# A two-model decoder kernel: VectorE's top-k laid in four parts between groups of four expert dots, and the next head's query matmuls laid between the value sets of an earlier sum

## Chip, cores and metric

One Trainium2 chip, one core of it. The metric is the time of one execution on the device in microseconds (us), lower is better. A change of this kernel under about 0.3% cannot be told from none.

## What is computed

A first model of two layers (attention, a pooling mixer and a PEER feed-forward) is followed by a second one of four layers (three kinds of attention and a squared-ReLU MLP). There are 256 tokens of width 1024, all in fp32. The change touches PEER alone, the product-key expert layer of the two first layers:

```python
def one_block(xblk):                                   # 128 tokens, two blocks
    q = (xblk @ w_query).reshape(B, 128, 8, 2, 256)    # 8 heads
    s = jnp.einsum('bthpd,hpnd->bthpn', q, sub_keys)   # 128 keys for each half
    vals, idx = lax.top_k(s, 16)
    cand = vals[..., 0, :, None] + vals[..., 1, None, :]      # 16 x 16
    cand_idx = idx[..., 0, :, None] * 128 + idx[..., 1, None, :]
    top_s, pos = lax.top_k(cand.reshape(B, 128, 8, 256), 16)
    eidx = jnp.take_along_axis(cand_idx.reshape(B, 128, 8, 256), pos, axis=-1)
    g = jax.nn.softmax(top_s, axis=-1)
    h = jnp.einsum('btd,bthkd->bthk', xblk, expert_u[eidx])
    act = jax.nn.gelu(h, approximate=False) * g
    return jnp.einsum('bthk,bthkd->btd', act, expert_v[eidx])
```

Each token, head and rank takes one row of `expert_u` and one of `expert_v`, 4 KB each.

## The kernel before, in words

The kernel is written engine by engine, with semaphores between them and all orders set by hand. Every engine takes its instructions in the order in which they are written.

PEER works in chunks. A chunk is one head h and one block t of 128 tokens, so a layer has 16 chunks; below, chunk c is 2h + t. The two chunks of a head use one half j of the buffers each, in a loop whose body holds two heads.

**GpSimd (POOL)** issues the gathers. `u_rows` (L1805) brings four U rows for each of the 128 tokens as four indirect DMAs of 512 KB; `v_rows` (L1818) does that for a V set of four ranks. The order is U group 0 of chunk c, V set 0 of chunk c-1, U group 1, V set 1 and so on: 32 gathers in a chunk. Only eight U buffers exist, so a U group waits until the dots of two groups earlier are done (`h_ready`). A V set waits until TensorE has used the same set of the chunk before (`v_free`).

**VectorE (DVE)** runs `dots`: 16 dots (L1575), each when its rows have landed; then it waits for ScalarE's exponential (`gate_ready`) and its gelu (`gelu_ready`), multiplies them (L1582), spreads the weights over the partitions (L1584, `rw_ready`) and copies the next index table (L1566). Then comes `topk` for the chunk two further on: for t = 0 a copy of the scores out of PSUM (L1520), two top-16 searches over 128 keys, the 16 x 16 sums and a top-16 search over them, and the arithmetic of the expert number (L1542 to L1552), which releases GpSimd's U rows of that chunk (`idx_ready`). At the end `stationaries` (L1597) builds the weight columns for TensorE out of `weights_by_pair`.

**TensorE (PE)** runs, for head h, `weights_by_pair` (L771) and `expert_sum` (L784, four sets of 16 matmul passes, each set when its V rows have landed) for t = 0, then `weights_by_pair` for t = 1, then `query` of head h+2, then `expert_sum` for t = 1. `query` transposes the sub-keys (L736), multiplies tokens by the head's query weights in four groups of 16 passes (L744), waits for ScalarE's copy of the result and makes the key scores (L751, `ps_done`).

**ScalarE (ACT)** runs `query_copies` (L1036 the transposed keys, L1038 the query after `q_done`) and `expert_weights` (L1044 the exponential, L1047 the gelu). `query_copies(h+1)` stands ahead of both `expert_weights` of head h, in one queue.

**SyncE (SP)** loads the query weights (2048 KB) and sub-keys (256 KB) of a head once those of two heads earlier are used.

Of the kernel before, what the change touches and what calls it, by code (L numbers as in the profile page):

```python
# [26 lines left out]
ALU = mybir.AluOpType  # L27
# [3 lines left out]
P = 128  # L31
D = 1024
S = 256
NT = S // P
KC = D // P
# [10 lines left out]
PH = 8  # L46
# [147 lines left out]
def program(nc, T, out):  # L194
    with ExitStack() as ctx:
# [354 lines left out]
        def _(pe):  # L550
# [110 lines left out]
            with pe.Fori(0, DEPTH) as l:  # L661
# [65 lines left out]
                def query(h, j, first):  # L727
# [12 lines left out]
                    for b in (2, 3, 0, 1):  # L740
                        if b == 0:
                            wait_loop(pe, sk_used, h + 1)
                        for k in range(KC):
                            mm = pe.matmul(psT[:, b // 2, (b % 2) * S:(b % 2 + 1) * S], ring[:, j, k, b * P:(b + 1) * P],  # L744
                                           xT[:, k, :], start=(k == 0), stop=(k == KC - 1))
                    mm.then_inc(q_done, 1)
# [7 lines left out]
                    mm.then_inc(ps_done, 1)  # L754

# [17 lines left out]
                def expert_sum(h, j, t, ahead=True):  # L773
# [4 lines left out]
                    for s in range(NSET):  # L778
# [8 lines left out]
                        mm.then_inc(v_free, 1)  # L787

                query(0, 0, True)
# [12 lines left out]
                query(1, 1, False)  # L802
                with pe.Fori(0, PH // 2 - 1) as hp:
                    for j in range(2):
                        weights_by_pair(2 * hp + j, j, 0)
                        expert_sum(2 * hp + j, j, 0)
                        weights_by_pair(2 * hp + j, j, 1)
                        query(2 * hp + 2 + j, j, False)
                        expert_sum(2 * hp + j, j, 1)
# [127 lines left out]
        def _(act):  # L937
# [61 lines left out]
            with act.Fori(0, DEPTH) as l:  # L999
# [49 lines left out]
                query_copies(0)  # L1049
                with act.Fori(0, PH // 2 - 1) as hp:  # L1050
                    query_copies(2 * hp + 1)
                    for t in range(NT):
                        expert_weights(2 * hp, 0, t)
                    query_copies(2 * hp + 2)
                    for t in range(NT):
                        expert_weights(2 * hp + 1, 1, t)
                query_copies(PH - 1)
# [127 lines left out]
        def _(dve):  # L1185
# [244 lines left out]
            with dve.Fori(0, DEPTH) as l:  # L1430
# [84 lines left out]
                def topk(h, j, t):  # L1515
                    cb = NT * j + t
                    restart_chain()
                    if t == 0:
                        wait_loop(dve, ps_done, h + 1)
                        link(dve.tensor_copy(topb[:, :, 0, :], psS[:, 1, :].rearrange("p (a n) -> p a n", n=NKEY)))  # L1520
                        dve.sem_inc(ps_used, 1)
                    for q in range(2):
                        top16(topb[:, 2 * t + q, 0, :], topb[:, 2 * t + q, 1, :], NKEY, vals[:, q, :], idxu[:, q, :])
                    link(dve.tensor_copy(idxf[:, :, :], idxu[:, :, :]))
# [11 lines left out]
                    link(dve.tensor_tensor(m(0), down(vals[:, 0, :]), along(vals[:, 1, :]), ALU.add))  # L1536
                    if not (isinstance(h, int) and h < 2):

                        wait_loop(dve, v_free, h * 8 + (4 * t - 8), alone=True)
                    top16(sc2[:, 0, :], sc2[:, 1, :], 256, tops[:, cb, :], posu[:, 0, :])  # L1540
                    link(dve.tensor_scalar(nmx[:, cb, :], tops[:, cb, 0:1], -1.0, None, ALU.mult))
# [26 lines left out]
                def dots(h, j, t, ahead=True):  # L1568
# [3 lines left out]
                    for k in range(TOPK):  # L1572
# [3 lines left out]
                                                 ALU.mult, ALU.add, hdot[:, cb, k:k + 1]).then_inc(h_ready, 1)  # L1576

# [8 lines left out]
                    if ahead:  # L1586
                        take_indices(c + 1, cb + 1)

# [21 lines left out]
                with dve.Fori(0, PH // 2 - 1) as hp:  # L1610
                    for j in range(2):
                        for t in range(NT):
                            dots(2 * hp + j, j, t)
                            topk(2 * hp + j + 1, 1 - j, t)
                            stationaries(2 * hp + j, j, t)
                for t in range(NT):
                    dots(PH - 2, 0, t)
                    topk(PH - 1, 1, t)
                    stationaries(PH - 2, 0, t)
                for t in range(NT):  # L1620
                    dots(PH - 1, 1, t, ahead=(t == 0))
# [237 lines left out]
```

## Time and profile before

| | |
|---|---|
| time, median of 3 runs | 3718.97 us (3710.23 to 3719.86) |
| the profiled execution: time, span | 3713.7 us, 3711.8 us |
| busy: PE, DVE, ACT, POOL | 2547.4, 2080.9, 827.9, 1119.8 us |
| DMA over the span | 884.64 MB, 238 GB/s |
| indirect gathers: instructions, bytes of their queue | 1024, 536.94 MB |
| first and last U gather, layer one | 343.74 us, 1068.05 us |
| first U gather, layer two | 1455.99 us |

The busy times are sums over stages that have nothing in common. Only the two PEER stages, some 750 us each, hold the work that is moved here; GpSimd has no instruction of weight outside them. So they are read by themselves, in windows and in the timelines of single engines. A row of a timeline gives the start, the duration, the engine, the line, the operation, its tiles and, in brackets, how long the engine stood idle before it and what ended that.

### The profile page before, as it was taken

To read this page: it belongs to the slowest core of one execution; us is meant where nothing else is said; L and a number is where in the kernel's file an instruction comes from. 1 tells how busy PE (TensorE), PEld (TensorE's weight loads), DVE (VectorE), ACT (ScalarE), POOL (GpSimd) and SP (SyncE) were. 2 spreads that over 40 slices of the span, in tenths; PEclk is the share of its full clock that TensorE was granted. 3 is DMA by queue.
4 is the path that set the end of the run, shared out by engine and by line. 5 is a ranking of instruction groups with operands and counts; after the bars stand their busy time and mean duration, and the time that the engine had idled before them with its cause. 6 is when DMAs were issued, how large, how long until landed. Compare 5 with 4: busy or idle time off the path is not lost.

```text
span 3711.8 us, 34410 instructions
## 1 busy us (share of the span) xinstructions
PE 2547.4 (69%) x12111; PEld 1746.3 (47%) x12111; DVE 2080.9 (56%) x4572; ACT 827.9 (22%) x1271; POOL 1119.8 (30%) x1028
## 2 busy tenths in 40 slices
PE   5986444444345986444444337799889979989898
PEld 2454222222002444222222005589778967977697
DVE  4544666667634545666666634655445554555554
ACT  0110100000000110100000004344434433444343
POOL 0001777677760001777777750000000000000000
PEclk9998776677556998776677568699969976998699
DMA  7723999999987713999999985145414531544153
GB/s 287 281 72 113 371 386 373 384 374 379 367 330 254 281 71 118 374 382 372 384 379 372 383 314 189 38 162 195 148 38 159 191 115 46 181 172 146 46 181 125
DMA packets 306600, 884.64 MB, mean 238 GB/s; under 512 B 21192, under 2 KB 31520, under 8 KB 306336
## 3 DMA queue, kind: packets, MB, share of 16 engines
q0 software_dynamic: 147456, 536.94, 37.9%
q1 hardware_dynamic: 159008, 346.05, 26.0%
q8 instruction: 66, 1.08, 0.1%
q14 instruction: 70, 0.57, 0.0%
HBM read 881.86 MB, written 1.05 MB: 238 GB/s over the span
## 4 chain that ended last, share of the span: by engine, by line
PE 48%; POOL 19%; DVE 13%; issue 13%; DMA 4%; ACT 2%; SPq 1%; DVEq 0%; POOLq 0%; ACTq 0%
POOL proj L1805 9%; PE lin L576 8%; PE lin L829 6%; PE lin L830 6%; PE lin L831 6%; POOL ring L1818 5%; POOL vbuf L1818 4%; PE psS L613 3%; DMA proj<-in_expert_u,eidx 2%; DVE proj L1575 2%; PE lin L642 2%; PE psT L556 2%; PE psT L829 2%; PE psT L830 2%; PE psT L831 2%
## 5 line engine op out<-in xcount | busy, mean ns | idle before, releaser
L1575 DVE CUSTOM_DVE_ANT_0 proj<-proj,tokb 128x1024 f32<-128x1024 f32 x512 | 611.1, 1224 | 410.9 <-DMA proj<-in_expert_u,eidx 384.7
L1805 POOL DMA_INDIRECT proj<-in_expert_u,eidx x512 | 545.1, 1065 | 927.3 <-DVEq L1553 704.9
L1282 DVE TENSOR_TENSOR weights_split<-ring,weights_split 128x1024 fp32r<-128x1024 f32 (+1 forms) x376 | 451.8, 1208 | 515.4 <-ACT weights_split L1093 514.9
L784 PE MATMUL lin<-ring,rowb 128*32 128x512 f32 x896 | 225.9, 1032 | 523.7 <-DMA ring<-in_expert_v,pT 302.8
L1093 ACT ACTIVATE weights_split<-ring 128x1024 fp32r<-128x1024 f32 (+1 forms) x376 | 391.7, 1046 | 570.3 <-PE lin L831 357.5
L784 PE MATMUL lin<-vbuf,rowb 128*32 128x512 f32 x1024 | 186.1, 871 | 260.4 <-DMA vbuf<-in_expert_v,pT 153.4
L784 PEld LDWEIGHTS lin<-ring,rowb 128*32 128x32 f32 x896 | 37.1, 157 | 669.2 <-DMA ring<-in_expert_v,pT 312.6
L576 PE MATMUL lin<-ring,xT 128*128 128x512 f32 x768 | 342.4, 607 | 5.6 <-DVE xT L1234 3.4
L1818 POOL DMA_INDIRECT vbuf<-in_expert_v,pT x256 | 293.1, 1145 | 78.1 <-issue 77.8
L1818 POOL DMA_INDIRECT ring<-in_expert_v,pT x224 | 249.3, 1113 | 68.3 <-issue 67.7
L576 PEld LDWEIGHTS lin<-ring,xT 128*128 128x128 f32 x768 | 148.8, 195 | 192.4 <-issue 184.7
L1047 ACT ACTIVATE gel<-hdot 128x16 f32<-128x16 f32 x32 | 6.9, 216 | 1013.1 <-DVE hdot L1575 1013.1
L744 PE MATMUL psT<-xT,ring 128*128 128x256 f32 x1024 | 228.9, 385 | 0.0
L829 PE MATMUL lin<-weights_split,act_split 128*128 128x512 f32 x512 | 202.6, 396 | 14.2 <-DVE act_split L1757 14.2
L744 PEld LDWEIGHTS psT<-xT,ring 128*128 128x128 f32 x1024 | 197.8, 195 | 27.1
L784 PEld LDWEIGHTS lin<-vbuf,rowb 128*32 128x32 f32 x1024 | 34.7, 139 | 370.4 <-DMA vbuf<-in_expert_v,pT 284.8
L830 PE MATMUL lin<-weights_split,act_split 128*128 128x512 f32 x512 | 201.9, 394 | 0.0
L831 PE MATMUL lin<-weights_split,act_split 128*128 128x512 f32 x512 | 201.9, 394 | 0.0
L829 PE MATMUL lin<-weights_split,xT_high 128*128 128x512 f32 (+1 forms) x480 | 190.4, 397 | 13.0 <-DVE xT_low L1299 7.4
L830 PE MATMUL lin<-weights_split,xT_low 128*128 128x512 f32 (+1 forms) x480 | 188.5, 393 | 0.0
L831 PE MATMUL lin<-weights_split,xT_high 128*128 128x512 f32 (+1 forms) x480 | 187.7, 391 | 0.0
L829 PE MATMUL psT<-xT_high,weights_split 128*128 128x256 f32 x512 | 148.8, 291 | 0.0
(236 smaller groups left out, 4590.8 us busy)
## 6 DMA issues: line engine op xcount, KB each, us to landing
ring<-in_mlp_w_up SPq DMA_DIRECT2D x32, 2048.0 KB, 8.1
ring<-in_mlp_w_down SPq DMA_DIRECT2D x32, 2048.0 KB, 7.6
ring<-in_ada_w SPq DMA_DIRECT2D x24, 2048.0 KB, 13.1
ring<-in_w_in SPq DMA_DIRECT2D x16, 2048.0 KB, 12.0
ring<-in_w_query SPq DMA_DIRECT2D x16, 2048.0 KB, 13.1
ring<-in_diff_w_in SPq DMA_DIRECT2D x12, 2048.0 KB, 8.0
ring<-in_moba_w_in SPq DMA_DIRECT2D x6, 2048.0 KB, 8.2
ring<-in_w_attn_o SPq DMA_DIRECT2D x4, 2048.0 KB, 11.7
```

Source lines behind the costliest of these rows:

```text
L576: mm = pe.matmul(lin[:, pair + t, 0:cols], lhs[:, k, t * P:(t + 1) * P], rhs[:, k, :], start=(k == 0), stop=(k == kc - 1))
L613: mm = pe.matmul(psS[:, g % 2, t * S:t * S + n], qkT[lo:hi, qb, t * P:(t + 1) * P], qkT[lo:hi, kb, 0:n], start=True, stop=True)
L744: mm = pe.matmul(psT[:, b // 2, (b % 2) * S:(b % 2 + 1) * S], ring[:, j, k, b * P:(b + 1) * P], xT[:, k, :], start=(k == 0), stop=(k == KC ...
L784: mm = pe.matmul(lin[32 * b:32 * b + 32, 2 * half + t, :], wst[:, cb % 2, 4 * b + s, :], vrow(SETROWS * s + b)[:, half * 512:(half + 1) * ...
L829: pe.matmul(out_ap, lhs[0], rhs[0], start=first, stop=False, skip_group_check=True)
L830: pe.matmul(out_ap, lhs[1], rhs[0], start=False, stop=False, skip_group_check=True)
L831: return pe.matmul(out_ap, lhs[0], rhs[1], start=False, stop=last, skip_group_check=True)
L1093: act.activation(part(p, 0, kind, w), raw_piece(slot, p, kind, w), ACT.Copy).then_inc(hi_ready, 1)
L1282: dve.tensor_tensor(part(p, 1, kind, w), raw_piece(slot, p, kind, w), part(p, 0, kind, w).bitcast(F32), ALU.subtract).then_inc(lo_ready, 1)
L1575: dve.tensor_tensor_reduce(ubuf[:, n % GB, :], ubuf[:, n % GB, :], tokb[:, t, :], 1.0, 0.0, ALU.mult, ALU.add, hdot[:, cb, k:k + 1]).then_ ...
L1805: pool.indirect_dma_start(out=ubuf[:, (16 * cb + k) % GB, :], out_offset=None, in_=table["u"], in_offset=bass.IndirectOffsetOnAxis(ap=eidx ...
L1818: pool.indirect_dma_start(out=vrow(SETROWS * s + b), out_offset=None, in_=table["v"], in_offset=bass.IndirectOffsetOnAxis(ap=eidxT[:, cb % ...
```

## The change

`topk` becomes `topk_part`, in four parts. Part 0 is the copy of the scores (t = 0 only) and the first search over 128 keys, part 1 the second search, part 2 the 16 x 16 sums with their search, part 3 the arithmetic of the expert number. `dots` calls part 0 after the 4th dot, part 1 after the 8th, part 2 after the 12th, and part 3 after the weights are spread. `query` becomes `query_keys`, `query_rows` in four parts and `key_scores`. The loop on TensorE calls `query_keys(h+2)` ahead of `expert_sum` of t = 0, one part of `query_rows` after each V set of that sum, and `key_scores` behind it: that is one chunk earlier than before. On ScalarE `query_copies(h+2)` moves between the two `expert_weights` of head h. GpSimd's and SyncE's orders stay as they are. The numbers of instructions and bytes stay too.

```diff
-                def query(h, j, first):
+                def query_keys(h, j):
...
-                    for b in (2, 3, 0, 1):
-                        if b == 0:
-                            wait_loop(pe, sk_used, h + 1)
-                        for k in range(KC):
-                            mm = pe.matmul(psT[:, b // 2, (b % 2) * S:(b % 2 + 1) * S], ring[:, j, k, b * P:(b + 1) * P],
-                                           xT[:, k, :], start=(k == 0), stop=(k == KC - 1))
-                    mm.then_inc(q_done, 1)
+
+                def query_rows(h, j, part):
+
+                    b = (2, 3, 0, 1)[part]
+                    if part == 2:
+                        wait_loop(pe, sk_used, h + 1)
+                    for k in range(KC):
+                        mm = pe.matmul(psT[:, b // 2, (b % 2) * S:(b % 2 + 1) * S], ring[:, j, k, b * P:(b + 1) * P],
+                                       xT[:, k, :], start=(k == 0), stop=(k == KC - 1))
+                    if part == 3:
+                        mm.then_inc(q_done, 1)
+
+                def key_scores(h):
+
                     wait_loop(pe, q_used, h + 1)
...
-                def expert_sum(h, j, t, ahead=True):
+                def expert_sum(h, j, t, ahead=True, asked=False):
...
                         mm.then_inc(v_free, 1)
+                        if asked:
+                            query_rows(h + 2, j, s)
...
                         weights_by_pair(2 * hp + j, j, 0)
-                        expert_sum(2 * hp + j, j, 0)
+                        query_keys(2 * hp + 2 + j, j)
+                        expert_sum(2 * hp + j, j, 0, asked=True)
+                        key_scores(2 * hp + 2 + j)
                         weights_by_pair(2 * hp + j, j, 1)
-                        query(2 * hp + 2 + j, j, False)
                         expert_sum(2 * hp + j, j, 1)
...
                 query_copies(0)
+                query_copies(1)
                 with act.Fori(0, PH // 2 - 1) as hp:
-                    query_copies(2 * hp + 1)
-                    for t in range(NT):
-                        expert_weights(2 * hp, 0, t)
-                    query_copies(2 * hp + 2)
-                    for t in range(NT):
-                        expert_weights(2 * hp + 1, 1, t)
-                query_copies(PH - 1)
+                    for j in range(2):
+                        expert_weights(2 * hp + j, j, 0)
+                        query_copies(2 * hp + 2 + j)
+                        expert_weights(2 * hp + j, j, 1)
...
                                                  ALU.mult, ALU.add, hdot[:, cb, k:k + 1]).then_inc(h_ready, 1)
+                        if ranked and k % 4 == 3 and k < 12:
+                            topk_part(h + 1, 1 - j, t, k // 4)
...
                     if ahead:
                         take_indices(c + 1, cb + 1)
+                    if ranked:
+                        topk_part(h + 1, 1 - j, t, 3)
...
                             dots(2 * hp + j, j, t)
-                            topk(2 * hp + j + 1, 1 - j, t)
                             stationaries(2 * hp + j, j, t)
```

How it moves instructions, in the order of each queue (an fp32 matmul is one row there and two passes in the profile, so x8 here is x16 there):

**ScalarE**, in the loop, from the gelu of block t = 0 to that of t = 1 and the query copies; `gel` is the gelu, `eg` the exponential, `sm<-psT` the copy of the query. Before:

```order
L1047 ACTIVATE gel<-hdot 128x16
L410 REGISTER_ALU
L1044 ACT_TABLE_LOAD
L1044 ACTIVATE eg,ers<-tops,nmx 128x16
L410 ISA
L1047 ACT_TABLE_LOAD
L1047 ACTIVATE gel<-hdot 128x16
L410 REGISTER_ALU
L1036 ACTIVATE pT<-psT 128x512
L1038 ACTIVATE sm<-psT 128x1024
```

The change:

```order
L1064 ACTIVATE gel<-hdot 128x16
L410 REGISTER_ALU x2
L1053 ACTIVATE pT<-psT 128x512
L1055 ACTIVATE sm<-psT 128x1024
L410 REGISTER_ALU
L1061 ACT_TABLE_LOAD
L1061 ACTIVATE eg,ers<-tops,nmx 128x16
L410 ISA
L1064 ACT_TABLE_LOAD
L1064 ACTIVATE gel<-hdot 128x16
```

The two copies, which followed the gelu of t = 1, now precede the exponential and the gelu of t = 1.

**TensorE**, in the loop, at the end of the sum of t = 0; `psT<-xT,ring` is the query, `lin<-...,rowb` a V set, `psS<-pT,sm` the key scores. Before:

```order
L771 MATMUL psS<-const,pT 128x16
L410 ISA
L736 MATMUL psT<-const,ring 128x128 x4
L410 REGISTER_ALU
L744 MATMUL psT<-xT,ring 128x256 x16
L410 REGISTER_ALU
L744 MATMUL psT<-xT,ring 128x256 x16
L751 MATMUL psS<-pT,sm 128x128 x8
L410 REGISTER_ALU
L784 MATMUL lin<-vbuf,rowb 32x512 x16
```

The change:

```order
L798 MATMUL lin<-ring,rowb 32x512 x8
L410 REGISTER_ALU
L747 MATMUL psT<-xT,ring 128x256 x8
L798 MATMUL lin<-ring,rowb 32x512 x3
L798 MATMUL lin<-pr,rowb 32x512
L798 MATMUL lin<-ring,rowb 32x512 x3
L798 MATMUL lin<-pr,rowb 32x512
L747 MATMUL psT<-xT,ring 128x256 x8
L758 MATMUL psS<-pT,sm 128x128 x8
L785 MATMUL psS<-const,pT 128x16
```

The last quarter of the query now follows the last V set of t = 0, and the weights of t = 1 (L785) follow the key scores.

**VectorE**, in the loop, from the 4th dot of t = 0 to the 5th; before, the 5th dot followed the 4th at once:

```order
L1598 ISA hdot 128x1
L1215 ISA
L410 REGISTER_ALU
L1539 COPY rope_t<-psS 128x4x128
L1524 MAX vals<-rope_t 128x8
L1525 MAX_INDEX idxu<-vals,rope_t 128x8
L1526 MATCH_REPLACE rope_t<-vals,rope_t 128x128
L1527 MAX vals<-rope_t 128x8
L1528 MAX_INDEX idxu<-vals,rope_t 128x8
L1598 ISA proj,hdot<-proj,tokb 128x1024
```

The copy of the scores has moved from behind the 16 dots to behind four of them.

## Rows read from the trace of the kernel before

**Rows 1.** Page, costliest groups: the dots and the U gathers.
```profile
L1575 DVE CUSTOM_DVE_ANT_0 proj<-proj,tokb 128x1024 f32<-128x1024 f32 x512 | 611.1, 1224 | 410.9 <-DMA proj<-in_expert_u,eidx 384.7
L1805 POOL DMA_INDIRECT proj<-in_expert_u,eidx x512 | 545.1, 1065 | 927.3 <-DVEq L1553 704.9
```
**Rows 2.** Busy time by windows (count), granted clock, DMA share, GB/s: two loops, one unranked chunk.
```profile
426.14:985.96 559.82, 260.50 (x1320) 123.31 (x1320) 374.44 (x931) 47.67 (x72) 423.76 (x384) 0.67 0.99 377
1042.79:1074.81 32.02, 10.92 (x48) 1.78 (x48) 18.29 (x31) 0.00 (x0) 24.70 (x25) 0.50 1.02 410
1554.60:2110.00 555.40, 256.24 (x1290) 118.78 (x1288) 373.45 (x929) 50.04 (x75) 422.17 (x384) 0.67 0.99 378
```
**Rows 3.** Line view of L1805, its wait for the dots, and of L1818, its landing times.
```profile
  DVE hdot L1575: 70.6, 12
...
DMA to landing us min/median/max: 5.2/6.5/12.9
```
**Rows 4.** Timeline of GpSimd, 547 to 662 us.
```profile
547.03 1.14 POOL L1805 DMA_INDIRECT proj<-in_expert_u,eidx  x1 [5.93 <-DVE hdot L1575]
...
578.41 0.97 POOL L1818 DMA_INDIRECT vbuf<-in_expert_v,pT  x1 [0.30 <-issue]
...
589.17 1.99 POOL L1818 DMA_INDIRECT vbuf<-in_expert_v,pT  x1 [0.30 <-issue]
...
615.74 0.99 POOL L1818 DMA_INDIRECT pr<-in_expert_v,pT  x1 [0.30 <-issue]
...
660.65 0.94 POOL L1818 DMA_INDIRECT pr<-in_expert_v,pT  x1 [0.31 <-issue]
```
**Rows 5.** Timeline of TensorE, 622 to 644 us: last set of t = 0, query, key scores.
```profile
622.81 1.07 PE L784 MATMUL lin<-ring,rowb 128*32 128x512 f32 x3 [9.29 <-DMA pr<-in_expert_v,pT]
...
626.95 13.98 PE L744 MATMUL psT<-xT,ring 128*128 128x256 f32 x64
642.04 2.05 PE L751 MATMUL psS<-pT,sm 128*128 128x128 f32 x16 [1.11 <-ACT sm L1038]
```
**Rows 6.** Timeline of ScalarE, 617 to 645 us.
```profile
617.23 0.22 ACT L1047 ACTIVATE gel<-hdot 128x16 f32<-128x16 f32 x1 [41.63 <-DVE hdot L1575]
...
640.97 1.02 ACT L1038 ACTIVATE sm<-psT 128x1024 f32<-128x1024 f32 x1 [13.22 <-PE psT L744]
642.01 1.28 ACT L1044 ACT_TABLE_LOAD   x1
643.30 0.31 ACT L1044 ACTIVATE eg<-tops,nmx 128x16 f32<-128x16 f32 x1
...
643.72 1.28 ACT L1047 ACT_TABLE_LOAD   x1
```
**Rows 7.** Timeline of VectorE, 572 to 588 us: weights, top-k from copy to end, dots.
```profile
572.72 0.23 DVE L1582 SCALAR_TENSOR_TENSOR actw<-eg,ers,gel 128x16 f32<-128x16 f32 x1 [0.30 <-ACT gel L1047]
...
573.28 0.69 DVE L1520 COPY rope_t<-psS 128x512 f32<-128x512 f32 x1
...
581.54 0.32 DVE L1542 TENSOR_SCALAR posu<-posu 128x16 uint32<-128x16 uint32 x1
...
586.24 0.68 DVE L1597 TENSOR_TENSOR rowb<-const,psS 128x512 f32<-128x512 f32 x1
586.84 1.22 DVE L1575 CUSTOM_DVE_ANT_0 proj<-proj,tokb 128x1024 f32<-128x1024 f32 x1
```
**Rows 8.** Timelines at the start of layer one's PEER: GpSimd.
```profile
363.81 1.68 POOL L1805 DMA_INDIRECT proj<-in_expert_u,eidx  x1 [10.21 <-DVE hdot L1575]
...
371.09 0.94 POOL L1805 DMA_INDIRECT proj<-in_expert_u,eidx  x1 [0.30 <-issue]
...
404.11 1.68 POOL L1805 DMA_INDIRECT proj<-in_expert_u,eidx  x1 [6.18 <-DVE hdot L1575]
```
**Rows 9.** Timeline of TensorE there: the key scores of head 1.
```profile
376.82 2.05 PE L751 MATMUL psS<-pT,sm 128*128 128x128 f32 x16 [1.11 <-ACT sm L1038]
```
**Rows 10.** Timeline of TensorE, 655 to 676 us: the last set of t = 1.
```profile
671.62 1.08 PE L784 MATMUL lin<-ring,rowb 128*32 128x512 f32 x3 [7.00 <-DMA pr<-in_expert_v,pT]
```

More of the change, by code:

```diff
@@ L754, in query @@
                     mm.then_inc(ps_done, 1)
+                def query(h, j):
+                    query_keys(h, j)
+                    for part in range(4):
+                        query_rows(h, j, part)
+                    key_scores(h)
                 def indices_by_pair(c, cb):
@@ L787, in expert_sum @@
                         mm.then_inc(v_free, 1)
-                query(0, 0, True)
+                        if asked:
+                            query_rows(h + 2, j, s)
+                query(0, 0)
                 for t in range(NT):
@@ L801, in _ @@
                 indices_by_pair(1, 1)
-                query(1, 1, False)
+                query(1, 1)
                 with pe.Fori(0, PH // 2 - 1) as hp:
@@ L1515, in topk, with topk_part @@
                 def topk(h, j, t):
+                    for part in range(4):
+                        topk_part(h, j, t, part)
+                def topk_part(h, j, t, part):
                     cb = NT * j + t
                     restart_chain()
-                    if t == 0:
+                    if t == 0 and part == 0:
                         wait_loop(dve, ps_done, h + 1)
@@ L1521, in topk @@
                         dve.sem_inc(ps_used, 1)
-                    for q in range(2):
+                    if part < 2:
+                        q = part
                         top16(topb[:, 2 * t + q, 0, :], topb[:, 2 * t + q, 1, :], NKEY, vals[:, q, :], idxu[:, q, :])
-                    link(dve.tensor_copy(idxf[:, :, :], idxu[:, :, :]))
+                        return
                     grid = [P, TOPK, TOPK]
@@ L1534, in m @@
                         return sc2[:, q, :].rearrange("p (a b) -> p a b", a=TOPK)
[L1536 to L1541, printed above, removed]
+                    if part == 2:
+                        link(dve.tensor_copy(idxf[:, :, :], idxu[:, :, :]))
+                        link(dve.tensor_tensor(m(0), down(vals[:, 0, :]), along(vals[:, 1, :]), ALU.add))
+                        if not (isinstance(h, int) and h < 2):
+                            wait_loop(dve, v_free, h * 8 + (4 * t - 8), alone=True)
+                        top16(sc2[:, 0, :], sc2[:, 1, :], 256, tops[:, cb, :], posu[:, 0, :])
+                        link(dve.tensor_scalar(nmx[:, cb, :], tops[:, cb, 0:1], -1.0, None, ALU.mult))
+                        return
                     link(dve.tensor_scalar(posu[:, 1, :], posu[:, 0, :], 4, None, ALU.logical_shift_right))
@@ L1566, in take_indices, with dots @@
                     dve.tensor_copy(eidxT[:, cb % 4, :], idx_at(cb)).then_inc(it_used, 1)
-                def dots(h, j, t, ahead=True):
+                def dots(h, j, t, ahead=True, ranked=True):
                     cb = NT * j + t
@@ L1617, in _ @@
                     dots(PH - 2, 0, t)
-                    topk(PH - 1, 1, t)
                     stationaries(PH - 2, 0, t)
                 for t in range(NT):
-                    dots(PH - 1, 1, t, ahead=(t == 0))
+                    dots(PH - 1, 1, t, ahead=(t == 0), ranked=False)
                     stationaries(PH - 1, 1, t)
```

## The prediction, made before the changed kernel ran

> **What bounds the kernel now.** I read the line groups of the page first, then windows over the two PEER loops, then the timelines of the single engines in one head. The page's busy shares mislead: they mix stages. The windows [rows 2] cut out chunks 2 to 13 of layer one, six heads, and as many gathers of layer two: 384 gathers each, in 559.82 and 555.40 us. The DMA share there is 0.99 at 377 GB/s, TensorE is busy for under half, VectorE for 67%. Two resources are near their end. One is DMA: in the chunk without top-k it moves 410 GB/s [rows 2], 1.28 us for a gather's 524 KB. A head brings 64 gathers, 2.10 MB of query weights and 0.26 MB of sub-keys, 35.9 MB, which at 410 GB/s take 87.6 us. The other is GpSimd, which issues the gathers one by one: 0.94 us and 0.30 us of "issue" [rows 4], 1.24 us each, 79.4 us a head. A head takes more than either:
>
> - layer one: 559.82 / 6 = 93.3 us. GpSimd's busy time is 423.76 - 384 x 0.94 = 62.8 us over plain issues, 10.5 a head. What is left after 384 x 0.30 is 20.9 us, 3.5 a head, in which it waits for dots.
> - layer two: 92.6 = 79.4 + 10.2 + 3.0, in the same way.
>
> So a head is 93.0 us: **79.4 of issues, 10.3 of stretched issues, 3.3 of waits**. GpSimd's queue is the path; all 12 of its waits for dots come to 70.6 us [rows 3].
>
> The stretches stand beside dots alone: the issue at 578.41 takes 0.97 us in the middle of the top-k, that at 589.17 takes 1.99 us after the dots have begun again at 586.84 [rows 4, 7]. They are worst when the top-k, 13 us in one piece (573.28 to 586.24) [rows 7], has let rows pile up and eight dots run on end. The waits come from that piece as well: 5.93 us at 547.03 [rows 4]. In the unranked chunk 25 issues hold only 24.70 - 25 x 0.94 = 1.2 us of stretch [rows 2], since there each dot follows its landing.
>
> **What the change does to it, part by part.**
>
> *Top-k in four parts.* No instruction is added but three restarts of the step counter a chunk, which hide in VectorE's idle third. Parts of 1.8 to 4.7 us after four dots of 4.6 us fit into the 10 us from one U group to the next, so in steady flow the dots keep to the landings. The waits for dots (3.3 us a head) go. The stretches fall, between two ends: not at all (10.3), and to the unranked chunk's rate, 1.2 / 25 x 64 = 3.1 us. I take 7.5. It is nearer the upper end because, as the next point shows, each head still has three groups of four dots run on end, and part 3 with the stationaries leaves one late group.
>
> The Trainium skill, SBUF — State Buffer, "Who interferes with whom", says that a VectorE instruction with two SBUF inputs contends with a GpSimd instruction that reads SBUF, and that the loser blocks for the whole instruction. The 1.99 us beside a 1.22 us dot agree with it [rows 4, 1]. Taken by itself it speaks against this change, since there are as many dots as before. That is the rival "stretches stay" below, and the unranked chunk is the row against it.
>
> *Query between the V sets, and ScalarE's queue.* Here I see the price. The exponential and the gelu of block t = 1 now stand behind the copy of the query of head h+2, which waits for the last quarter of the query, which stands behind the last V set of t = 0. That set's gathers are issued after the last U group of t = 1. So VectorE finishes the 16 dots of t = 1 and stands at `gate_ready`. Counted from the end of the last V issue (615.74 + 0.99 = 616.7 [rows 4]):
>
> 1. the set begins at 622.81 [rows 5]: 6.1 us. Bounds: 5.2 us from issue to landing at the least [rows 3], so 4.2, and 671.62 - 661.6 = 10.0 [rows 10, 4];
> 2. set: 3.6 us (622.81 to about 626.4); quarter of the query: 13.98 / 4 = 3.5 us at 2.4 GHz [rows 5]. A set of 3.6 us goes with a granted clock of 0.50, 1.2 GHz, in the unranked chunk [rows 2], so the quarter begins at that level: I add 0.5. Sum 7.6; bounds 5.3 (both at 2.4 GHz) and 10.6 (both at 1.2 GHz);
> 3. ScalarE: from 640.93, the query's end, to the end of a gelu behind it: copy 1.02, table load 1.28, exponential with its accumulator 0.4, table load 1.28 (from 643.72), gelu 0.22 [rows 6]: 4.3 us. Before, the gelu was at 617.23, right after the last dot;
> 4. VectorE: weights 0.56 (572.72 to 573.28), part 3 4.7 (581.54 to 586.24), stationaries 0.6, four dots 4.6 [rows 7]: 10.5 us. Then 0.2 us to GpSimd.
>
> Together 28.7 us. GpSimd meanwhile has two U groups and two V sets to issue, 16 x 1.24 + 0.3 = 20.1 us, with some stretch 20.8; its third U group of the next chunk needs those four dots. **It waits 7.9 us, once a head**, for heads 0 to 5, whose sums carry a query: six times a layer. Bounds: 4.2 + 5.3 + 15.0 - 20.8 = 3.7 us, and 10.0 + 10.6 + 15.0 - 20.8 = 14.8 us. I take 7.9, the values of one head's own rows.
>
> The same rows weigh a rule. In them the exponential starts at 643.30, directly behind its load of 1.28 us [rows 6]. The Trainium skill, ScalarE: Activation LUTs, "What ACT_TABLE_LOAD costs", adds a drain of 1380 ns to each. By it the two loads of step 3 would cost 2.8 us more a head, 33 us in all; the row shows no drain, and my sum has none.
>
> After the wait VectorE works off its arrears: copy of the scores and part 0, part 1 and part 2 with four dots each. GpSimd's next third of a head is 20 us long, so I find no second wait. The key scores are ready about 17 us after the reference point, before part 0 asks. `weights_by_pair` of t = 1 falls into part 3. SyncE's query load starts some 10 us earlier than before and is wanted 90 us later: nothing.
>
> Head: 79.4 + 7.5 + 7.9 = 94.8 us, against 93.0: **+1.8 x 12 = +21.6 us**.
>
> *The start of a layer.* Part 0 for head 1 now follows the first four dots, while TensorE ends the key scores of head 1 only at 376.82 + 2.05 = 378.9 [rows 9]. The four dots are done at 363.5, as GpSimd's release at 363.81 shows [rows 8]. VectorE waits 15 us; copy, part 0 and four dots end at 386.3. GpSimd's fourth U group, at 371.1 before, comes at 386.4. From there: group 0 of chunk 1 after part 1 and four dots (392.8), V set 0, group 1 (402.8), V set 1, to 412.9 for group 2, which stood at 404.11 and there still had a wait of 6.18 us in it [rows 8]. +8.8 us a layer, **+17.6 us**.
>
> *The end of a layer.* Some one and a half ranked chunks with no wait, before and after: 3 us less stretch a layer, **-6 us**.
>
> Sum: 21.6 + 17.6 - 6 = +33 us. The profiled execution took 3713.7 us (span 3711.8), 5 us under the median of the runs and inside their spread. That gives **3747 us**, +0.9%. A change under about 0.3% (11 us) a measurement of this kernel cannot tell from none.
>
> **Rivals.**
>
> - *Faster: the flow smooths out.* If TensorE, busier and more even, keeps 2.4 GHz, the set and quarter take 5.3 us; if also the last set begins nearer its minimum, the wait is about 5.0, and with stretches at 5.0 a head is 89.4, still over DMA's 87.6. Then 12 x -3.6 + 17.6 - 6 = -32: 3682 us. It decides once wait and stretch together are under 11.7 us a head. For it: the unranked chunk, and 13 us in one piece gone. Against: ScalarE's order.
> - *No change.* TensorE at 2.4 GHz alone: wait 5.6, head 92.5, 12 x -0.5 + 11.6 = +6: 3719 us.
> - *Stretches stay* at 10.3: head 97.6, +67: 3780 us. For it: no dot is gone, and arrears make bursts.
> - *TensorE stays at 1.2 GHz* through the query quarter: 3.0 us more wait, head 97.8, +69: 3783 us; with the last set as late as in rows 10, 3.9 more each, 3830 us. Against: the granted clock is up in every query of the timeline.
> - *The drain of the page* on top: 3780 us, though the trace has none.
>
> **How the numbers follow.** Forecast (3747, by itself 3725 to 3770) 0.31; smooth flow 0.26; no change 0.17; stretches stay 0.15; low clock 0.08; drain 0.03. Faster 0.26, within 0.3% 0.17, slower 0.57. For 8 in 10 the range reaches down towards the smooth case and up over the two cases at 3780: 3688 to 3800 us.
>
> **What would show it.** In the profile after: GpSimd waits for dots about six times a layer, some 8 us each, always ahead of the third U group of an even chunk; VectorE waits some 10 us for ScalarE's gate or gelu after the last dot of odd chunks; on ScalarE the exponential directly follows the query copy; mean issue 1.05 us where it is 1.10; U group 3 of chunk 0 some 15 us late in each layer. Wrong if the gelu of odd chunks comes within 2 us of the last dot, if GpSimd has no such waits, or if its issues are stretched as before.

## The result, and the profile after

| | before | after |
|---|---|---|
| time, median | 3717.95 us | 3787.95 us (4 runs, 3781.62 to 3792.93) |
| ratio, 95% interval | 1 | 1.0193 [1.0175, 1.0212] |
| profiled execution: time, span | 3713.7, 3711.8 us | 3792.9, 3791.0 us |

Slower, as forecast, but by 70 us where 33 were worked out (3747 us); the range up to 3800 us holds it. The page after, costliest groups, beside [rows 1]:

```profile
L1830 POOL DMA_INDIRECT proj<-in_expert_u,eidx x512 | 533.6, 1042 | 1035.1 <-DVEq L1576 700.5
L1598 DVE CUSTOM_DVE_ANT_0 proj<-proj,tokb 128x1024 f32<-128x1024 f32 x512 | 611.4, 1224 | 243.0 <-DMA proj<-in_expert_u,eidx 212.0
```

The U issues got shorter (1042 ns for 1065) and their idle time grew by 108 us. The window over chunks 2 to 13 of layer one, columns as in [rows 2]:

```profile
439.00:1025.64 586.64, 268.43 (x1272) 116.72 (x1270) 369.33 (x929) 50.27 (x75) 409.06 (x385) 0.70 0.95 359
```

By this window a head takes 97.8 us where it took 93.3; the DMA share is down from 0.99 to 0.95, and the granted clock is up from 0.67 to 0.70. The view of waits lists for whom GpSimd waits (total us, times, longest):

```profile
POOL proj L1830 <- DVE hdot L1598: 184.5, 18, 17.7
POOL proj L1830 <- issue: 150.1, 492, 0.3
```

Its waits for dots grew from 70.6 us [rows 3] to 184.5. I cut GpSimd's timeline into the start of a layer (first gather to U group 2 of chunk 1), six heads (to U group 2 of chunk 13) and the rest. Stretch is what the issues take over 0.94 us; wait is what a head takes beyond its stretch and 64 x 1.24 us:

| us, layer one / two | before | after | forecast of the difference |
|---|---|---|---|
| start | 60.4 / 59.4 | 74.3 / 74.2 | +8.8 |
| a head | 93.05 / 93.0 | 98.0 / 97.8 | +1.8 |
| of it stretch | 10.2 / 10.6 | 8.2 / 7.9 | -2.8 |
| of it wait | 3.5 / 3.0 | 10.4 / 10.5 | +4.6 |
| rest | 131.1 / 129.2 | 124.9 / 129.9 | -3 |

Heads bring +58.5 us (forecast 21.6), starts +28.7 (17.6), rests -5.5 (-6). Together 81.7, of which the span shows 79.2.

The hold that was forecast, VectorE standing still for ScalarE's exponential and gelu, is there as described. VectorE, GpSimd, TensorE and ScalarE around the end of chunk 5, each from its own timeline:

```profile
636.76 1.23 DVE L1598 CUSTOM_DVE_ANT_0 proj<-proj,tokb 128x1024 f32<-128x1024 f32 x1
...
650.47 0.16 DVE L1605 RECIPROCAL ers<-ers 128x1 f32<-128x1 f32 x1 [12.48 <-ACT eg L1061]
651.88 0.23 DVE L1607 SCALAR_TENSOR_TENSOR actw<-eg,ers,gel 128x16 f32<-128x16 f32 x1 [1.25 <-ACT gel L1064]
...
657.42 1.22 DVE L1598 CUSTOM_DVE_ANT_0 proj<-proj,tokb 128x1024 f32<-128x1024 f32 x1
```

```profile
635.38 0.93 POOL L1843 DMA_INDIRECT pr<-in_expert_v,pT  x1 [0.31 <-issue]
...
662.89 0.93 POOL L1830 DMA_INDIRECT proj<-in_expert_u,eidx  x1 [6.71 <-DVE hdot L1598]
```

```profile
641.89 0.63 PE L798 MATMUL lin<-ring,rowb 128*32 128x512 f32 x3 [1.75 <-DMA pr<-in_expert_v,pT]
...
643.75 3.72 PE L747 MATMUL psT<-xT,ring 128*128 128x256 f32 x16
648.58 2.05 PE L758 MATMUL psS<-pT,sm 128*128 128x128 f32 x16 [1.11 <-ACT sm L1055]
```

```profile
647.50 1.02 ACT L1055 ACTIVATE sm<-psT 128x1024 f32<-128x1024 f32 x1 [45.60 <-PE psT L747]
648.54 1.28 ACT L1061 ACT_TABLE_LOAD   x1
649.84 0.31 ACT L1061 ACTIVATE eg<-tops,nmx 128x16 f32<-128x16 f32 x1
...
651.55 0.22 ACT L1064 ACTIVATE gel<-hdot 128x16 f32<-128x16 f32 x1
```

But GpSimd's wait is not the same in each head. In layer one it is 6.68 and 6.71 us at chunks 2 and 6, 8.13 at 10 and 12, and twice as much at chunks 4 and 8: 16.30 and 16.34 us. Two of them, at chunks 4 and 10:

```profile
568.35 0.94 POOL L1830 DMA_INDIRECT proj<-in_expert_u,eidx  x1 [16.30 <-DVE hdot L1598]
...
860.95 0.94 POOL L1830 DMA_INDIRECT proj<-in_expert_u,eidx  x1 [8.13 <-DVE hdot L1598]
```

From the end of the last V issue to the end of the gelu 15.5 to 17.2 us pass in each of the twelve heads. From there to the gather it is 19.3 to 19.5 us at chunks 4 and 8 of both layers, and 10.8 to 11.4 us at the other eight. Chunk 4, VectorE's timeline:

```profile
554.11 0.68 DVE L1624 TENSOR_TENSOR rowb<-const,psS 128x512 f32<-128x512 f32 x1
560.14 1.22 DVE L1598 CUSTOM_DVE_ANT_0 proj<-proj,tokb 128x1024 f32<-128x1024 f32 x1 [5.35 <-issue]
...
565.10 0.08 DVE L1598 DVE_READ_ACCUMULATOR2_ANT hdot<- 128x1 f32 x1 [2.58 <-issue]
```

"issue" means that VectorE waited for nothing that the profile shows. At chunk 6 the dots follow the stationaries at once (657.42 above); here 5.35 and 2.58 us pass without an instruction. Chunks 4 and 8 open the second and the third pass of VectorE's loop over pairs of heads. The kernel before had the first gap at the same place, but not the second: its dots run on end.

```profile
541.55 1.23 DVE L1575 CUSTOM_DVE_ANT_0 proj<-proj,tokb 128x1024 f32<-128x1024 f32 x1 [5.33 <-issue]
```

The first four dots end at 546.2 and release the wait of 5.93 us at 547.03 that [rows 4] show, which I had put down to the top-k.

### The profile page after: what moved, and what is told of

The parts are those of the page before. It is cut to its first block, busy times and chain, and to the rows that moved or that the text cites. A ratio compares the mean times of both kernels' runs of the same rounds, so it can differ in the third digit from the quotient of the medians.

```text
span 3791.0 us, 34574 instructions
## 1 busy us (share of the span) xinstructions
PE 2584.4 (68%) x12111; PEld 1752.9 (46%) x12111; DVE 2071.3 (55%) x4572; ACT 828.6 (22%) x1271; POOL 1089.5 (29%) x1028
## 4 chain that ended last, share of the span: by engine, by line
PE 49%; POOL 20%; issue 14%; DVE 11%; DMA 3%; ACT 2%; SPq 0%; POOLq 0%; DVEq 0%; ACTq 0%
POOL proj L1830 9%; PE lin L576 8%; POOL ring L1843 6%; PE lin L846 6%; PE lin L847 6%; PE lin L848 6%; POOL vbuf L1843 4%; PE psT L747 3%; PE psS L613 3%; DMA pr<-in_expert_v,pT 2%; PE lin L642 2%; PE psT L556 2%; PE psT L846 2%; PE psT L847 2%; PE psT L848 2%
## 5 line engine op out<-in xcount | busy, mean ns | idle before, releaser
L1830 POOL DMA_INDIRECT proj<-in_expert_u,eidx x512 | 533.6, 1042 | 1035.1 <-DVEq L1576 700.5
L798 PE MATMUL lin<-ring,rowb 128*32 128x512 f32 x896 | 216.5, 994 | 446.2 <-DMA ring<-in_expert_v,pT 258.8
L798 PE MATMUL lin<-vbuf,rowb 128*32 128x512 f32 x1024 | 214.6, 988 | 320.8 <-DMA vbuf<-in_expert_v,pT 264.7
L576 PE MATMUL lin<-ring,xT 128*128 128x512 f32 x768 | 338.5, 601 | 5.8 <-DVE xT L1249 3.4
L798 PEld LDWEIGHTS lin<-ring,rowb 128*32 128x32 f32 x896 | 36.0, 150 | 569.1 <-DMA ring<-in_expert_v,pT 267.3
L1843 POOL DMA_INDIRECT vbuf<-in_expert_v,pT x256 | 262.6, 1026 | 78.1 <-issue 77.8
L1843 POOL DMA_INDIRECT ring<-in_expert_v,pT x224 | 261.8, 1169 | 68.3 <-issue 68.3
L747 PE MATMUL psT<-xT,ring 128*128 128x256 f32 x1024 | 253.6, 405 | 0.0
L747 PEld LDWEIGHTS psT<-xT,ring 128*128 128x128 f32 x1024 | 204.9, 205 | 102.2 <-issue 73.8
L798 PEld LDWEIGHTS lin<-vbuf,rowb 128*32 128x32 f32 x1024 | 37.3, 153 | 440.2 <-DMA vbuf<-in_expert_v,pT 304.2
L576 PEld LDWEIGHTS lin<-ring,xT 128*128 128x128 f32 x768 | 147.3, 193 | 190.0 <-issue 182.3
```

What stands on the lines that cost most here:

```text
L576: mm = pe.matmul(lin[:, pair + t, 0:cols], lhs[:, k, t * P:(t + 1) * P], rhs[:, k, :], start=(k == 0), stop=(k == kc - 1))
L798: mm = pe.matmul(lin[32 * b:32 * b + 32, 2 * half + t, :], wst[:, cb % 2, 4 * b + s, :], vrow(SETROWS * s + b)[:, half * 512:(half + 1) * ...
L1830: pool.indirect_dma_start(out=ubuf[:, (16 * cb + k) % GB, :], out_offset=None, in_=table["u"], in_offset=bass.IndirectOffsetOnAxis(ap=eidx ...
L1843: pool.indirect_dma_start(out=vrow(SETROWS * s + b), out_offset=None, in_=table["v"], in_offset=bass.IndirectOffsetOnAxis(ap=eidxT[:, cb % ...
```

## The experiments

Theory: the loss is the hold by ScalarE's queue, the gap at the loop, which the hold leaves bare, and the start of a layer. Rivals: the parts of the top-k themselves, or TensorE's new order, slow the flow. Nine kernels ran in twelve runs on three chips: a1 to a4 on the first, the b runs on the second, the c runs on the third. Ratios are to the kernel before on the same chip, which took 3907.6 us on the first (9 runs, 3884 to 3927.5), 3726.7 on the second and 3719.1 on the third. So the first is called the slow chip below. Three of its four kernels were run again on the third chip (c1 to c3). The changed kernel was not run again beside them; where it is compared with a run, its ratio of 1.0193 stands for it.

### Each half of the change alone

`a3_topk_parts_only`, `c2_topk_parts_only`: VectorE's part of the diff alone, TensorE and ScalarE as before.

```diff
 # VectorE as changed; TensorE's and ScalarE's hunks taken back:
-                        query_keys(2 * hp + 2 + j, j)
-                        expert_sum(2 * hp + j, j, 0, asked=True)
-                        key_scores(2 * hp + 2 + j)
+                        expert_sum(2 * hp + j, j, 0)
                         weights_by_pair(2 * hp + j, j, 1)
+                        query(2 * hp + 2 + j, j, False)
                         expert_sum(2 * hp + j, j, 1)
```

> VectorE's order of the change alone; TensorE's and ScalarE's orders as before the change. Theory: no hold at the gate, the layer's start still 14 us late, part 0 now waits for key scores that come late in even chunks (VectorE 3 to 10 us, GpSimd some 3 us a head), stretches 8 us a head instead of 10.3: 3716 us (3700 to 3740). Rival: the parts of the top-k are themselves the loss (VectorE late to the landings): 3770 us or more.

> VectorE's order of the change alone, TensorE and ScalarE as before. Theory: the top-k parts between the dots cost nothing by themselves and the hold of the scaling by the query copies is absent or short, so only the loop's branch gap and what is left of the hand-over show: GpSimd's wait for the first dot 3 to 6 us a head, 3715 to 3745 us, ratio 0.999 to 1.008. Rival: laying the top-k in parts is itself the loss; then the wait is 8 us or more and the ratio 1.010 or more (1.0127 stood on the other chip).

`a4_query_parts_only`, `c3_query_parts_only`: the other half.

```diff
 # TensorE and ScalarE as changed; VectorE's hunks taken back:
-                        if ranked and k % 4 == 3 and k < 12:
-                            topk_part(h + 1, 1 - j, t, k // 4)
...
                             dots(2 * hp + j, j, t)
+                            topk(2 * hp + j + 1, 1 - j, t)
```

> TensorE's and ScalarE's orders of the change alone; the top-k in one piece behind the dots, as before. Theory: the hold at the gate stays and the piece behind it is 8.3 us longer, so GpSimd waits some 16 us a head, 24 at a loop's end: 3890 us (3850 to 3920), with no loss at a layer's start. Rival: the query's place is harmless and the parts were the loss: within 15 us of 3718 us.

> TensorE's and ScalarE's order of the change alone, VectorE's top-k in one piece as before. Theory: the top-k of the chunk waits for a query that now ends at the last V set and stands ahead of the dots in one piece, so each head waits 20 us or more: 3850 to 3950 us, ratio 1.035 to 1.06 (1.0497 on the other chip), with no loss at the start of the layer. Rival: the copies are early enough and the top-k is hidden behind the gathers in flight; then 3740 us or less.

Measured: the top-k parts alone 3720.99 us, ratio 1.0007 [0.9993, 1.0022] (slow chip 1.0127 [1.0065, 1.0189]); the query parts alone 3854.5 us, 1.0377 [1.0357, 1.0396] (slow chip 1.0497 [1.0408, 1.0587]). By the cuts of the table above, the first has heads of 91.95 and 92.0 us, 1.0 less than before, and starts of 74.3 and 74.5, 14 more. So the parts win 13 us in the twelve heads and 7 us in the rests, against 29 us that they lose at the two starts; the time does not differ clearly from that of the kernel before. VectorE waits there for the key scores of a query that still comes late, 184.5 us in 16 waits, where the kernel before has 35.5 us in 2. The second has starts of 60.7 and 60.5 as before, and heads of 104.9 and 105.1. Its VectorE:

```profile
650.57 0.16 DVE L1595 RECIPROCAL ers<-ers 128x1 f32<-128x1 f32 x1 [12.98 <-ACT eg L1061]
651.98 0.23 DVE L1597 SCALAR_TENSOR_TENSOR actw<-eg,ers,gel 128x16 f32<-128x16 f32 x1 [1.25 <-ACT gel L1064]
...
664.19 0.68 DVE L1612 TENSOR_TENSOR rowb<-const,psS 128x512 f32<-128x512 f32 x1
664.79 1.22 DVE L1590 CUSTOM_DVE_ANT_0 proj<-proj,tokb 128x1024 f32<-128x1024 f32 x1
```

The same hold, and behind it some 12 us of top-k before the stationaries and the next dot, where the changed kernel has 4.6 (652.15 to 656.8): GpSimd waits 13 to 19 us a head. So the loss is the query's half; the top-k's parts take half of it back (1.0377 to 1.0193). The range expected of `c3_query_parts_only`, 3850 to 3950 us, held, but at its lower end: the waits stayed under the 20 us or more a head that it was worked out from. That of `c2_topk_parts_only` held too. `a4_query_parts_only` fits its range when scaled (1.0497 x 3718 = 3903 us), `a3_topk_parts_only` does not: on the slow chip the top-k parts alone came out as a loss.

### The gelu ahead of the query's copy

`a1_gelu_first`, `c1_gelu_first`: the changed kernel, ScalarE's order mended.

```diff
-                query_copies(0)
-                query_copies(1)
+                for h in range(2):
+                    query_copies(h)
+                    query_rows_copy(h)
...
                         query_copies(2 * hp + 2 + j)
                         expert_weights(2 * hp + j, j, 1)
+                        query_rows_copy(2 * hp + 2 + j)
```

`query_copies` here copies the transposed keys alone, `query_rows_copy` the query.

> The changed kernel, with ScalarE's copy of the query rows put behind the exponential and the gelu of t = 1 (the copy of the sub-keys stays ahead of them). Theory: the hold of VectorE at the gate is the main loss. Then the gelu comes within 1 us of the last dot in odd chunks, GpSimd's six waits a layer fall from 6.7 to 8.1 us to 0 to 2 us, and the two of 16 us at the end of a loop turn to some 8 us; the time falls by about 75 us to 3710 us (3695 to 3730). Rival: the loss sits in the four-part top-k and the layer's start; then at most 20 us are gained, 3770 us or more.

> The changed kernel with ScalarE's gelu of the second token moved between the two copies of the query (as in a1, on another chip now). Theory: the gelu comes right behind the last dot, VectorE's scaling no longer waits 12 to 14 us behind PSUM copies, but the last quarter of the query now also stands behind it; the wait for the first dot of a head falls from 10.4 to about 7 us only if TensorE's sets do not slip. 3710 to 3745 us, ratio 0.998 to 1.007. Rival (what the other chip showed, ratio 1.0157): TensorE's single passes slow down in this arrangement whatever the chip; then the wait for the first dot is over 12 us and the ratio above 1.012.

Measured on the third chip: 3714.82 us, 0.9994 [0.9983, 1.0005]: 74 us under the changed kernel by the ratios, and near the 3710 us first expected. VectorE no longer waits for `eg`. In the view of VectorE's waits, after:

```profile
DVE ers L1605 <- ACT eg L1061: 168.6, 12, 15.2
DVE rowb L1624 <- PE psS L785: 72.0, 18, 7.6
```

with the gelu first:

```profile
DVE rowb L1628 <- PE psS L785: 179.5, 30, 10.2
```

Much of that time is now waited one step later, for TensorE's `weights_by_pair` of t = 1, which still stands behind the last quarter: 179.5 us, where the two waits together were 240.6. And some 5 us of VectorE's arrears, part 3 of the top-k, are worked off ahead of it. GpSimd's waits of over 1 us from chunk 2 to 13 of layer one:

```profile
557.50 0.94 POOL L1834 DMA_INDIRECT proj<-in_expert_u,eidx  x1 [11.68 <-DVE hdot L1602]
...
742.19 0.94 POOL L1834 DMA_INDIRECT proj<-in_expert_u,eidx  x1 [11.29 <-DVE hdot L1602]
829.18 0.93 POOL L1834 DMA_INDIRECT proj<-in_expert_u,eidx  x1 [1.15 <-DVE hdot L1602]
917.79 0.94 POOL L1834 DMA_INDIRECT proj<-in_expert_u,eidx  x1 [1.16 <-DVE hdot L1602]
```

The waits of the heads within a pass are gone to about 1 us; those at chunks 4 and 8 stay, at 11.68 and 11.29 us, where some 8 were expected. That separates the hold from the gap.

On the slow chip the same kernel came to 3953.75 us, 1.0157 [1.0108, 1.0207], a loss where a gain was expected. There TensorE had idle time with no releaser; its view of waits:

```profile
PE lin L798 <- issue: 74.9, 42, 7.8
PE psT L747 <- issue: 57.8, 43, 2.2
```

On the third chip the same instructions of the same kernel show none (L747: 249.2 us busy, 0.0 idle). The gaps of `a3_topk_parts_only` on the slow chip are of the same kind (92.2 us, 56 times, ahead of L744). So ratios of that chip mix this in, and I draw no size from them. What caused it was not tried, nor whether these gaps are what the loss consists of: `a2_gelu_and_weights_first` below has more of them (119.2 and 88.9 us at the same two lines) and is faster.

### The weights ahead of the last quarter too

```diff
                         if asked:
+                            if s == 3:
+                                weights_by_pair(h, j, 1)
                             query_rows(h + 2, j, s)
...
                         key_scores(2 * hp + 2 + j)
-                        weights_by_pair(2 * hp + j, j, 1)
                         expert_sum(2 * hp + j, j, 1)
```

> As a1, and on TensorE the weights of t = 1 stand ahead of the last quarter of the query, so that the stationaries of t = 1 need not wait for the key scores. Theory: some 1 us a head more than a1, 12 us, 3700 us. Rival: the weights hidden under part 3 already, then the same as a1 within 5 us.

This is on top of the gelu's order. Measured, on the slow chip alone: 3877.67 us (8 runs), 0.9926 [0.9887, 0.9965], against 1.0157 for the gelu alone. That is 76 us where 12 were expected; the size was missed, and on this chip it is no measure. The direction is what the wait of 179.5 us says. On the other chips it ran only in the combinations below. There the two profiles give a hint of its size: heads of 91.3 and 92.0 us with the gelu alone (`c1_gelu_first`), 89.1 and 88.5 with the weights and the start as well (`b5_all_looped`), some 34 us over the twelve heads.

### The loop of VectorE written out

```diff
-                with dve.Fori(0, PH // 2 - 1) as hp:
+                for hp in range(PH // 2 - 1):
```

> The changed kernel with VectorE's loop over pairs of heads written out three times (same instructions, no branch back). Theory: the 5.4 and 2.6 us in which VectorE issues nothing at the head of the second and third pass come from the branch back; without it GpSimd's two waits of 16 us a layer become 8 us, and the time falls by about 32 us to 3756 us. Rival 1: the gaps belong to something else at that place (a wait the profile does not name) and stay: 3788 us. Rival 2: code written out is fetched with gaps elsewhere: 3788 us or more, gaps at other rows.

> The kernel before with VectorE's loop written out. Theory: its 5.3 us gaps at the same places (four of them) sat inside GpSimd's waits of 5.9, 5.9, 5.7 us; without them 10 to 20 us less, 3700 us. Rival: the 13 us top-k made those waits alone: 3718 us within 6 us.

Measured: the changed kernel without the loop 3759.3 us, 1.0083 [1.0054, 1.0112], 41 us less by the ratios (32 expected; the two intervals, added as squares, leave 28 to 54). The two profiled executions differ by 29 us, their heads by 30. VectorE has no such gap any more, and GpSimd's waits at chunks 2 to 8 of layer one read

```profile
465.20 0.94 POOL L1830 DMA_INDIRECT proj<-in_expert_u,eidx  x1 [9.02 <-DVE hdot L1598]
557.84 0.94 POOL L1830 DMA_INDIRECT proj<-in_expert_u,eidx  x1 [6.68 <-DVE hdot L1598]
654.32 0.94 POOL L1830 DMA_INDIRECT proj<-in_expert_u,eidx  x1 [9.04 <-DVE hdot L1598]
749.51 0.94 POOL L1830 DMA_INDIRECT proj<-in_expert_u,eidx  x1 [6.68 <-DVE hdot L1598]
```

6.68 us at chunk 4 instead of 16.30. So the gap belongs to the loop; what the engine does in it no row tells. The kernel before without its loop: 3717.76 us, 0.9979 [0.9962, 0.9995], some 8 us less (2 to 14), under the 10 to 20 expected. There the gap falls where other arrears take its place: GpSimd's waits stay at 69.5 us, 13 times, instead of 70.6, 12 times, and the heads of its profile are no shorter (93.4 and 93.6 us).

### The start of a layer

```diff
+                query_keys(1, 1)
+                for part in range(3):
+                    query_rows(1, 1, part)
+                indices_by_pair(0, 0)
+                indices_by_pair(1, 1)
+                query_rows(1, 1, 3)
+                key_scores(1)
                 for b in range(4):
                     mm = pe.matmul(lin[:, b, :], ident, cst("zero"), start=True, stop=False, skip_group_check=True)
                 pe.sem_inc(v_free, NSET)
-                indices_by_pair(0, 0)
-                indices_by_pair(1, 1)
-                query(1, 1)
```

> The changed kernel; at a layer's start TensorE runs the query of head 1 in two pieces ahead of and behind the two index matmuls, and zeroes the sums last, so that the key scores of head 1 are ready some 13 us earlier. Theory: VectorE's wait of 15 us at part 0 falls to about 2, GpSimd's of 17.7 us to about 4, 12 us a layer: 3764 us. Rival: the dots of chunk 0 are bound by the index copy then (it needs TensorE in the same span): 3780 us or more.

Measured: 3776.54 us, 1.0129 [1.0097, 1.0162], 24 us less by the ratios, as expected (10 to 38 by the two intervals). VectorE's copy of the scores of head 1, after and here:

```profile
377.23 0.69 DVE L1539 COPY rope_t<-psS 128x512 f32<-128x512 f32 x1 [15.03 <-PE psS L758]
```

```profile
365.08 0.69 DVE L1543 COPY rope_t<-psS 128x512 f32<-128x512 f32 x1 [2.40 <-PE psS L758]
```

The wait falls from 15.03 to 2.40 us, the start from 74.3 and 74.2 to 64.0 and 64.0. The heads do not gain: they come to 99.1 and 98.6 us, 1 us over the 98.0 and 97.8 of the changed kernel, and the two profiled executions differ by 11 us only.

### Everything together

`b5_all_looped` has the two orders of ScalarE and TensorE and the start; `c4_all_unrolled` has the written-out loop as well.

> a2 and b3 together. Theory: the parts add up: 3788 - 75 - 12 - 24 = 3677 us (3660 to 3695), faster than the kernel before by about 40 us; DMA's 87.6 us a head is then near. Rival: once GpSimd does not wait, DMA bounds the heads and half of the gain is given back: 3700 us or more.

> All corrections in one: gelu and weights of the second token first, start of the layer put back in its order, VectorE's loop over pairs of heads written out three times. Theory: beside the same with the loop (ratio 0.9828) it takes the gap without an instruction of 5.4 and 2.6 us out of four heads; there the waits were 1.8 to 2.9 us in the mean, so at most 12 to 20 us more: 3640 to 3655 us, ratio 0.978 to 0.982. Rival: the gap is hidden by gathers in flight now; then 3660 to 3668 us. Second rival: the longer program costs VectorE's instruction supply elsewhere; then slower than with the loop.

| | time | ratio | head, layers one / two | GpSimd's waits for dots |
|---|---|---|---|---|
| with the loop | 3664.08 us | 0.9828 [0.9792, 0.9863] | 89.1 / 88.5 us | 62.6 us |
| written out | 3649.3 us | 0.9819 [0.9803, 0.9836] | 87.4 / 88.0 us | 45.4 us |

Both times lie in the ranges expected. Both kernels beat the changed one and the one before, the latter by 1.7 and 1.8%. Whether writing out the loop still brings anything, the two intervals do not tell; the heads of the two profiles differ by 1.7 and 0.4 us, 13 us over the twelve. The windows of the written-out one over chunks 2 to 13 of both layers:

```profile
426.88:950.67 523.79, 264.08 (x1281) 118.71 (x1279) 372.62 (x931) 47.31 (x71) 400.54 (x384) 0.72 1.02 402
1524.78:2051.21 526.43, 257.06 (x1236) 110.03 (x1236) 373.90 (x926) 46.29 (x70) 407.09 (x384) 0.71 1.02 400
```

The DMA share is 1.02 at 400 GB/s, and a head takes 87.3 and 87.7 us by the windows: the 87.6 us that DMA needs by [rows 2]. But GpSimd's own queue is nearly full as well: in layer one 79.4 us of plain issues and 6.7 of stretch leave 1.3 us of waits in a head of 87.4, and most of the 45.4 us stands at the starts. Which of the two binds is not shown. That no order of the queues would gain more in the loop is argued from the share, not tried.

## Why the prediction was off: each step

**The hold** was right in mechanism, and in size up to small parts. At the end of chunk 5, from the end of the last V issue at 636.31: set at 641.89, 5.6 us (forecast 6.1); set and quarter to 647.47, 5.6 (7.6); ScalarE 4.3 (4.3); VectorE 10.3 (10.5); from the last dot to the gather 0.8 (0.2, a term that I had taken from no row). Together 26.6, and GpSimd had 19.9 us of its own work (20.8): 6.7 us of wait, as the row says. In this head the set ran at a granted clock of 1.00, 2.4 GHz, four rows of 0.6 us. That is the exception. Ahead of chunk 10 the four rows take 0.63, 0.80, 1.09 and 1.09 us at a mean granted clock of 0.60, and in ten of the twelve heads set and quarter take 6.9 to 7.3 us, near the forecast. The eight waits of this kind come to 61.2 us, 7.65 each; forecast 7.9. That the mean comes so close owes something to terms that err both ways (0.6 us too little to the gather, 0.8 too much of GpSimd's own work). Taking the hold away (`c1_gelu_first`) gave 74 us back, and left the gap.

**The step that failed** is the last one of the sum for the hold, step 4: VectorE's path. It takes VectorE from the stationaries straight into four dots in every head, 10.5 us, and puts what may lie between them at nothing. In two heads of six the loop over pairs goes back there, and nothing issues for 5.35 and then 2.58 us. The hold had used up all of the slack, so these 8 us go to GpSimd in full, not as the second wait that the prediction looked for, but as a part of the same one: 16.30, 16.34, 16.72 and 14.93 us, 64.3 in place of 31.6. That is +32.7 us; `b1_after_unrolled` gave back 41 (28 to 54). The row of 5.33 us stood in the timeline of before, inside a wait that I put down to the top-k ("The waits come from that piece as well"). There it costs some 8 us in all, 2 to 14 (`b2_before_unrolled`). So the same 5 us are nearly free in one order and dear in the other. The 2.58 us within the second dot were not to be read from before: `c1_gelu_first`, `c2_topk_parts_only`, `b3_start` and `b5_all_looped` have them too, all with the top-k in parts and the loop, and `c3_query_parts_only`, with the top-k in one piece, has not.

**Start of a layer.** The mechanism was right and its first half exact: VectorE waits 15.03 us (15), and U group 3 of chunk 0 comes 42.8 us after the first gather (384.85 against 342.04; forecast 42.7). Mis-sized was the path from there to group 2 of chunk 1: 74.3 us after the first gather, not 69.2. I had gone by issues with next to no stretch. VectorE works off its arrears there with dots end to end, and issues stretch, in GpSimd's timeline:

```profile
388.81 1.98 POOL L1830 DMA_INDIRECT proj<-in_expert_u,eidx  x1 [0.30 <-issue]
...
397.00 1.99 POOL L1843 DMA_INDIRECT vbuf<-in_expert_v,pT  x1 [0.30 <-issue]
...
407.64 1.99 POOL L1830 DMA_INDIRECT proj<-in_expert_u,eidx  x1 [0.30 <-issue]
```

The 20 issues from U group 3 of chunk 0 on take 5.8 us more than plain ones, in both layers. Together the starts cost 28.7 us for 17.6, +11. `b3_start` takes 10.3 and 10.2 us of the start back.

**Stretches** fell from 10.4 to 8.1 us a head, by 2.3 where 2.8 were forecast: +5 us over twelve heads. So the rival "stretches stay" was wrong, and with it my reading of the Trainium skill, SBUF — State Buffer, "Who interferes with whom", that I set beside it. The rule speaks of what contends, not of how often: as many dots stand here, and the stretch goes from 10.4 to 8.1, and to 6.7 in layer one of `c4_all_unrolled`.

**The drain.** In ScalarE's rows above the exponential starts at 649.84, where its load ends at 649.82. The Trainium skill, ScalarE: Activation LUTs, "What ACT_TABLE_LOAD costs", has 1380 ns of drain beside the load; no run here shows it, and the 1.28 us of the load itself is right.

**The smooth flow** did not come, but not because it is impossible: `c4_all_unrolled` is that case, with heads of 87.4 and 88.0 us. ScalarE's order stood against it, as forecast (`c1_gelu_first`); so did TensorE's order and the start.

In sum 49 of the 82 us were not in the forecast: the gap +33, the other eight waits -2, stretches +5, starts +11; the rest is rounding and the ends of the layers. The range held the time for two reasons that had nothing to do with the gap: it was drawn up to 3800 us for stretches that stay and for a low clock, and neither came so. That part was luck.

## What to carry to other kernels

When an order makes one engine's queue the path, every stall of that queue that was hidden comes into the open. So list the rows with "issue" as their releaser on the engine that will be on the path, see whether they stand where a loop goes back, and add them to the sum. An instruction moved into another engine's queue takes on the waits that stand ahead of it: here one copy, which could wait, held up a gelu that the next 16 gathers hung on. And a split of work is worth judging in the order that it then lands in: the same two splits cost 1.9%, and with three orders around them mended they gain 1.7%.

## What the runs showed of the hardware

- In the changed kernel VectorE issues nothing for 5.35 to 5.43 us where its loop goes back (929 timed instructions in chunks 2 to 13, which are three passes long), and for 2.52 to 2.62 us again within the second dot. In the kernel before the first gap takes 4.50 to 5.33 us and the second is absent. Both are gone with the body written out (`b1_after_unrolled`, `b2_before_unrolled`, `c4_all_unrolled`). Why they are there no row tells.
- Three chips ran the kernel before in 3908, 3727 and 3719 us. On the slow one the profile of `a1_gelu_first` has some 130 us of TensorE gaps with no releaser in the PEER stages (L798 and L747), which that of `c1_gelu_first`, the same kernel on the third, has not; matmuls elsewhere took as long on both (L576: 338.3 and 340.4 us). The ratios of three kernels differed too between these two chips, by 1.2 to 1.6%. A ratio from one chip is not a ratio for all; the cause stays open.
- From the end of the dot's accumulator read to the start of the gather that waits for it 0.8 us pass (662.08 to 662.89), in before as well (546.22 to 547.03).
